# Decoder step with expert retrieval: two expert tables joined into one, gathered once a slot, and value rows weighted by diagonal matrices on TensorE

## The reference

```python
q = (xb @ w_q).reshape(PEER_BLOCK, PEER_HEADS, 2, PEER_DHALF).astype(F32)
s = jnp.einsum('nhpd,hpkd->nhpk', q, keys)
top_s, top_i = lax.top_k(s, PEER_TOPK)
...
idx = jnp.take_along_axis(cand_idx, best_j, axis=-1)
gsm = jax.nn.softmax(best_s, axis=-1)
act = jax.nn.gelu(jnp.einsum('nd,nhkd->nhk', xb, expert_u[idx]).astype(F32))
wts = (gsm * act).astype(xb.dtype)
return jnp.einsum('nhk,nhkd->nd', wts, expert_v[idx])
```

## Time and profile before

| | before |
|---|---|
| median of 3 runs | 2366.38 us (2363.53 to 2371.35) |
| span of the profiled execution | 2366.5 us |
| PE busy | 1659.4 us, 70% |
| DVE busy | 1552.5 us, 66% |
| ACT busy | 594.8 us, 25% |
| POOL busy | 1386.6 us, 59% |
| moved by DMA | 730.57 MB, of it 604.58 MB by the gathers |

### The profile page before, as it was taken

The page is one execution under the profiler, slowest core; times in us unless marked ns, Lnnn a source line. Parts: engine busy times, 40 slices in busy tenths (PEclk is TensorE's granted clock), DMA queues, the critical chain, the costliest instruction groups (busy, mean ns, idle before and its releaser), DMA issues. The chain is left out here.

```text
span 2366.5 us, 16881 instructions
## 1 busy us (share of the span) xinstructions
PE 1659.4 (70%) x4628; PEld 841.7 (36%) x4628; DVE 1552.5 (66%) x3174; ACT 594.8 (25%) x777; POOL 1386.6 (59%) x1231
## 2 busy tenths in 40 slices
PE   7999977888799999867754544555445556555545
PEld 3799863344345555523311111121111112111111
DVE  2450289989785666586777787587777556556554
ACT  1161222222642212322222222121222112221212
POOL 0000026565557776556666666766677886777784
PEclk9999998999799999887876666566666656765578
DMA  8766578999789999788988888988888988899996
GB/s 274 248 206 213 181 280 314 334 334 349 275 318 382 397 395 383 281 298 306 344 317 296 315 303 301 314 310 303 318 289 316 325 319 328 319 327 346 332 322 236
DMA packets 286556, 730.57 MB, mean 309 GB/s; under 512 B 22187, under 2 KB 135220, under 8 KB 286333
## 3 DMA queue, kind: packets, MB, share of 16 engines
q0 software_dynamic: 166032, 604.58, 70.5%
q1 hardware_dynamic: 119188, 123.91, 15.9%
q10 hardware_dynamic: 1250, 1.09, 0.2%
HBM read 726.43 MB, written 3.06 MB: 308 GB/s over the span
## 5 line engine op out<-in xcount | busy, mean ns | idle before, releaser
L689 PE MATMUL v_sum<-t_v_rows,t_ident 128*128 128x512 f32 (+1 forms) x1152 | 819.0, 853 | 649.2 <-DVE t_v_rows L1303 648.5
L479 POOL DMA_INDIRECT t_u_rows<-in_expert_u,t_step_idx x576 | 673.8, 1170 | 468.2 <-POOLq L478 336.5
L479 POOL DMA_INDIRECT t_v_rows<-in_expert_v,t_step_idx x576 | 681.7, 1184 | 178.3 <-issue 161.1
L1303 DVE SCALAR_TENSOR_TENSOR t_v_rows<-t_v_rows,t_wts 128x1024 f32<-128x1024 f32 x288 | 370.1, 1285 | 474.8 <-ACT t_v_rows L859 471.8
L689 PEld LDWEIGHTS v_sum<-t_v_rows,t_ident 128*128 128x128 f32 (+1 forms) x1152 | 266.0, 252 | 1156.5 <-DVE t_v_rows L1303 905.2
L859 ACT ACTIVATE t_v_rows<-t_v_rows,t_wts 128x1024 f32<-128x1024 f32 x288 | 330.5, 1147 | 1347.6 <-DMA t_v_rows<-in_expert_v,t_step_idx 1318.8
L601 PE MATMUL bank<-t_arena,t_weights 128*128 128x192 f32 (+1 forms) x2560 | 646.6, 411 | 8.2 <-issue 5.0
L601 PEld LDWEIGHTS bank<-t_arena,t_weights 128*128 128x128 f32 x2560 | 454.0, 192 | 205.3 <-issue 60.2
L1277 DVE CUSTOM_DVE_ANT_0 t_u_rows<-t_u_rows,t_arena 128x1024 f32<-128x1024 f32 x384 | 459.0, 1224 | 24.4 <-DMA t_u_rows<-in_expert_u,t_step_idx 20.5
L1277 DVE CUSTOM_DVE_ANT_0 t_u_rows<-t_u_rows,t_tok 128x1024 f32<-128x1024 f32 x192 | 227.9, 1222 | 10.2 <-DMA t_u_rows<-in_expert_u,t_step_idx 8.0
L470 POOL COPY t_step_idx<-t_idx 128x16 uint32<-128x16 uint32 x24 | 9.5, 421 | 308.9 <-DVEq L1263 308.8
(11 more groups left out here) (166 smaller groups left out, 910.8 us busy)
## 6 DMA issues: line engine op xcount, KB each, us to landing
t_weights<-in_w_in SPq DMA_DIRECT2D x40, 1024.0 KB, 6.0
t_weights<-in_w_ada SPq DMA_DIRECT2D x24, 1024.0 KB, 5.4
t_weights<-in_w_q SPq DMA_DIRECT2D x16, 1024.0 KB, 7.6
t_u_rows<-in_expert_u,t_step_idx POOLq DMA_INDIRECT x576, 6.2
t_v_rows<-in_expert_v,t_step_idx POOLq DMA_INDIRECT x576, 6.3
t_weights<-in_w_branch_a SPq DMA_DIRECT2D x8, 1024.0 KB, 10.5
t_weights<-in_w_branch_b SPq DMA_DIRECT2D x8, 1024.0 KB, 10.9
t_weights<-in_w_out SPq DMA_DIRECT2D x8, 1024.0 KB, 11.6
```

The lines of the kernel that those rows point to most:

```text
L479: pool.indirect_dma_start(out=rows[:, k % slots, :], out_offset=None, in_=source, in_offset=bass.IndirectOffsetOnAxis(ap=step_idx[:, table ...
L689: nc.tensor.matmul(v_sum[0:m, half], add, row[:, half], start=False, stop=False).then_inc(v_free, 1)
L1303: V.scalar_tensor_tensor(out=two, in0=one, scalar=wts[:, k:k + 1], in1=two, op0=ALU.mult, op1=ALU.add).then_inc(paired_done, 1)
```

## The change

`expert_u` and `expert_v` are joined on the host to one table of 16384 rows of 2048 floats (8 KB). One gather brings u and v of a slot into one of `NSLOT` = 8 buffers of 8 KB a partition, so 576 gathers take the place of 1152, and the 64 KB that the buffers take in a partition stand against 48 KB before (the scratch for DMA descriptors is set to 4096 B). There is no fetching of u a step ahead. For each pair DVE makes two dots and nothing else; ACT makes gelu of 2 numbers, two products with `gsm`, and two diagonal matrices (identity times weight) that are written over the used u rows; PE multiplies each v row by its diagonal matrix, so four matmuls of 128x512 a pair instead of two. The multiply-and-add on DVE (L1303), ACT's scaling of a row (L859) and DVE's `weigh` are gone. The stages of the dots ahead of stage A are gone as well; some units that stood ahead of the first pair (queries 12 to 15, the rows of tile 1, a norm, two choices) now stand in the first places of stage A, and the load of the second group's x is issued by ACT.

```diff
-NW, NU, NV, NBANK = 3, 4, 8, 6
+NW, NSLOT, NBANK = 3, 8, 6
...
-    start += [[u] for u in queries[:5] + [key, queries[5], pair] + queries[6:8] + [number] + queries[8:10]
-              + [key1, queries[10], dot[0], queries[11], pair1, queries[12], queries[13], queries[14], queries[15],
-                 ("tok", 1, 0), square, dot[1], number1, norm, ("ada", 0, 22), dot[2], key2, ("ada", 0, 23), dot[3], pair2]]
+    start += [[u] for u in queries[:5] + [key, queries[5], pair] + queries[6:8] + [number, queries[8], queries[9], key1, queries[10], queries[11], pair1]]
...
+    places[0] += [queries[12], number1]
+    places[1] += [queries[13], queries[14]]
+    places[2] += [queries[15], ("tok", 1, 0)]
+    places[3] += [square, key2]
+    places[4] += [norm]
...
+        uv_rows = sb("uv_rows", [P, NSLOT, 2 * D])
...
+        def diag_of(t, k):
+
+            return uv_rows[:, k % NSLOT, 0:NS if t == 0 else P]
...
+            def fetch_step(t, i, number, odd, first):
+
+                nc.gpsimd.tensor_copy(step_idx[:, odd, :], idx_of(t)[:, bass.ds(i * TOPK, TOPK)]).then_inc(idx_copied, 1)
+                pool.wait_ge(idx_copied, number + 1)
+                for k in range(TOPK):
+                    if k >= NSLOT or not first:
+
+                        pool.wait_ge(slot_free, 1)
+                        pool.sem_inc(slot_free, -1)
+                    pool.indirect_dma_start(
+                        out=uv_rows[:, k % NSLOT, :], out_offset=None, in_=A["expert_uv"],
+                        in_offset=bass.IndirectOffsetOnAxis(ap=step_idx[:, odd, k:k + 1], axis=0),
+                    ).then_inc(uv_in[k % NSLOT], 16)
...
+            def sum_pair(t, number, j):
                 m = rows_of(t)
-                add = ident2[:, :] if t == 0 else ident[:, :]
-                for j in pairs:
-                    pe.wait_ge(paired_done, number * PAIRS + (j + 1))
-                    row = v_rows[:, (2 * j + 1) % NV, :]
-
-                    for half in (slice(0, 512), slice(512, D)):
-                        nc.tensor.matmul(v_sum[0:m, half], add, row[:, half], start=False, stop=False).then_inc(v_free, 1)
+                pe.wait_ge(diag_done, number * PAIRS + (j + 1))
+                for k in (2 * j, 2 * j + 1):
+                    nc.tensor.matmul(v_sum[0:m, 0:512], diag_of(t, k), v_row(k)[:, 0:512], start=False, stop=False)
+                    nc.tensor.matmul(v_sum[0:m, 512:D], diag_of(t, k), v_row(k)[:, 512:D], start=False, stop=False).then_inc(slot_free, 1)
...
+            def weigh(t, number, j):
+
+                p = number * PAIRS + (j + 1)
+                two = slice(2 * j, 2 * j + 2)
+                act.wait_ge(dots_done, p)
+                nc.scalar.activation(gelus[:, two], dots[:, two], ACT.Gelu_apprx_tanh).then_inc(gelu_done, 1)
+                act.wait_ge(gelu_done, p)
+                nc.scalar.activation(wts[:, 2 * j:2 * j + 1], gelus[:, 2 * j:2 * j + 1], ACT.Copy, scale=step_gsm[:, 2 * j:2 * j + 1])
...
+                nc.scalar.activation(diag_of(t, 2 * j), one, ACT.Copy, scale=wts[:, 2 * j:2 * j + 1])
+                nc.scalar.activation(diag_of(t, 2 * j + 1), one, ACT.Copy, scale=wts[:, 2 * j + 1:2 * j + 2]).then_inc(diag_done, 1)
...
-                one, two = v_rows[:, k % NV, :], v_rows[:, (k + 1) % NV, :]
-                dve.wait_ge(v_in[k % NV], number * (16 * TOPK // NV) + 16 * (k // NV + 1))
-                dve.wait_ge(scaled_done, number * PAIRS + (j + 1))
-                V.scalar_tensor_tensor(out=two, in0=one, scalar=wts[:, k:k + 1], in1=two, op0=ALU.mult, op1=ALU.add).then_inc(paired_done, 1)
+                dve.sem_inc(gsm_done, 1)
+
+            def pair(t, number, j):
+
+                for k in (2 * j, 2 * j + 1):
+                    dve.wait_ge(uv_in[k % NSLOT], number * (16 * TOPK // NSLOT) + 16 * (k // NSLOT + 1))
+                    ins = V.tensor_tensor_reduce(out=u_row(k), in0=u_row(k), in1=h2_rows(t), scale=1.0, scalar=0.0, op0=ALU.mult, op1=ALU.add,
+                                                 accum_out=dots[:, k:k + 1])
+                ins.then_inc(dots_done, 1)
```

More of the change, by code:

```diff
@@ L176, in schedule @@
     places = [[] for _ in range(PAIRS * len(steps))]
-    later = [number2] + [u for t, y in ((0, 3), (1, 0), (1, 1), (1, 2), (1, 3)) for u in choice_units(t, y)]
-    deal(later, places, 0, CHOICE_PLACES)
-    spread(copied, places, 0, CHOICE_PLACES)
+    places[0] += [queries[12], number1]
[3 more added lines that the diff above has]
+    places[4] += [norm]
+    later = [("ada", 0, 22), pair2, ("ada", 0, 23), number2] + [u for t, y in ((0, 3), (1, 0), (1, 1), (1, 2), (1, 3)) for u in choice_units(t, y)]
+    deal(later, places, 5, CHOICE_PLACES)
+    spread(copied, places, 6, CHOICE_PLACES)
     queries, (key, pair, number) = query_units(1), choice_units(2, 0)
@@ L190, in between @@
             if after:
-                close = j == PAIRS - 1 and i == TILE_STEPS[t] - 1
-                return [("sum", "pair", t, (i, j))] + [("both", "final", t, 0)] * close
-            return [("pair", "pair", t, (i, j))] + [("both", "final", t - 1, j + 1)] * (t > 0 and i == 0 and j < 3)
+                return [("sum", "pair", t, (i, j))]
+            return [("pair", "pair", t, (i, j))] + [("both", "final", t - 1, j)] * (t > 0 and i == 0 and j < 4)
         return between
@@ L198, in schedule @@
     for t in group_tiles(1):
-        last = TILE_STEPS[t] - 1
+        last = TILE_STEPS[t]
         if PEELED[t]:
@@ L211, in schedule @@
             s += [("both", "loop", t, (PEELED[t], last))]
-        s += staggered([[] for _ in range(PAIRS)], pair_entries([(t, last)]))
-    s += [("both", "final", t, stage) for stage in (1, 2, 3)]
+    s += [("both", "final", t, stage) for stage in range(4)]
     return s
@@ L363, in trunk @@
         dve_step, coef_done, idx_done, rates_done = (sem(x) for x in ("dve_step", "coef_done", "idx_done", "rates_done"))
[L364 to L367 removed]
+        uv_in = [sem(f"uv_in{i}") for i in range(NSLOT)]
+        gsm_done, gsm_copied, idx_copied, dots_done, gelu_done, wts_done, diag_done, slot_free = (sem(x) for x in (
+            "gsm_done", "gsm_copied", "idx_copied", "dots_done", "gelu_done", "wts_done", "diag_done", "slot_free"))
         v_tile, v_read, yfin, ysq, ymean, ystd, yready, tails, out_done = (sem(x) for x in (
@@ L511, in _ @@
                     number = STEP0[t] + i
-                    after = following(t, i)
-                    if after and after[1] % (TILE_STEPS[after[0]] // 4) == 0:
-                        pool.wait_ge(idx_done, 4 * after[0] + 1 + 4 * after[1] // TILE_STEPS[after[0]])
-                    fetch_step(after, (t, i), number % 2, number)
+                    if i % (TILE_STEPS[t] // 4) == 0:
+                        pool.wait_ge(idx_done, 4 * t + 1 + 4 * i // TILE_STEPS[t])
+                    fetch_step(t, i, number, number % 2, number == 0)
                 if kind == "loop":
@@ L694, in _ @@
                     with pe.Fori(0, end - first) as i:
-                        sum_pairs(g, i + (STEP0[g] + first), range(PAIRS))
+                        for j in range(PAIRS):
+                            sum_pair(g, i + (STEP0[g] + first), j)
                 elif kind == "final":
@@ L1330, in _ @@
                         for j in range(PAIRS):
-                            pair(g, i + first, i + (STEP0[g] + first), j, g)
+                            pair(g, i + (STEP0[g] + first), j)
                 elif role == "pair":
-                    i, j = b
-                    next_tile = g if i + 1 < TILE_STEPS[g] else g + 1 if g + 1 < TILES else None
-                    pair(g, i, STEP0[g] + i, j, next_tile)
+                    pair(g, STEP0[g] + b[0], b[1])
                 elif role in ("make", "sum"):
                     continue
-                elif kind == "dots":
-                    for k in quarter(b):
-                        dot(0, 0, k)
                 elif kind == "ada":
```

121 lines of the change are left out of this document (31 added, 90 removed).

## The result

The changed kernel takes 2182.36 us (median of 4 runs, 2181.82 to 2185.64) against 2368.38 (4 runs) for the kernel before: a ratio of 0.9225, 95% interval 0.9203 to 0.9246, so 7.75% faster. The prediction said 2243, 5.2% faster. The profiled execution has a span of 2180.4 us.

The account below looks back on a forecast made before the run. POOL's gather issue was taken to bound stage B, PE and DVE stage A. After the change: 325 (start) + 861 (stage A) + 1036 (stage B) + 21 (end) = 2243 us, range 2120 to 2385 for 8 in 10.

Parts of the forecast that it names:

- What bounds stage B: In the last 192 pairs of the kernel before, POOL's gather issue was the bound: 199 of 205 us for 32 pairs.
- Stage B, 1036 us: The last 192 pairs: 991 us at the DMA engines' pace, plus 45 us for choices and queries.
- 5.16 us a pair: DMA pace for the last 192 pairs, the middle of 5.30 (396 GB/s) and 5.02 (418 GB/s).
- The choices: Choices and queries lengthen the last 192 pairs by 45 us, between 0 and 53, through DVE and the loading of weights.
- Stage A, 861 us: Pairs 0 to 95: PE's 827 us of work at a busy share of 0.96, between 827 and 950 us.
- Start and end: The first pair's sum stands at about 325 us; 21 us follow the last transfer's end.
- POOL's issue, 1.47 us: An 8 KB-row gather costs POOL 1.17 + 0.30 us as before, 2.9 us a pair; upper bound 2.64 us each.
- The ring: In the last 192 pairs each of eight buffers is held 15 to 17 us, where 20.6 are allowed.
- The rival of 23.6 us: Buffers held 23.6 us would set the pace of the last 192 pairs at 5.9 us each; total 2385 us; chance 0.13.
- The clock: In the last 192 pairs TensorE was counted on at 2.4 GHz; the sign was a PE clock above 0.85.
- The rival of 2659 us: TensorE stays at half clock: eight records take 7.56 us a pair in the last 192 pairs; chance 0.08.
- 358 GB/s: Rival: transfers in the last 192 pairs go no faster, 5.86 us a pair; total 2377 us, no gain; chance 0.05.

Follow-up runs that it names:

- light engines: The change with two 4 KB gathers a slot and each dot over half its row: 2296.75 us; with the value sum's right half also left out: 2191.49 us.
- the short gather at every second slot: The change, plus a second gather of 16 rows of 64 bytes, read by nothing, behind every second slot: 2197.05 us.

## Why the prediction was right, point by point

The direction, the places and the mechanism held; the sum was 61 us too high.

- **What bounds stage B.** Right, and shown by two steps that keep the 8 KB rows: POOL held by a filler takes back most of what one gather a slot gains (50 of 69 us in the last three parts), a second gather at every other slot, with POOL not full, next to none of it (4 us). One part of the argument was too simple: the prediction let the halved count do all of it, but 131 of the 250 us came with two gathers a slot still issued. In the one part with pairs alone that was compared, POOL's busy time fell by 20.8 us and the part by 18.6, so there it is POOL's time, by shorter issues (152.1 to 135.4 us) and fewer copies of indices (7.1 to 2.9); that the missing addition shortened the issues is likely, but no run took the addition alone away. The row that the prediction read on this was off by a little: that issue ended 0.82 us after the dot, not its full 0.94.
- **Stage B, 1036 us, measured 1014.** The mis-sized term is the pace, 5.16 us a pair: the parts of pairs alone, (156.7 + 164.4 + 156.6)/95.5, give 5.00, by the bound of 5.02 that the earlier trace rows gave for gathers alone. A short burst without other traffic was the better row, because that is what stage B then consists of. The choices cost 1014 - 191.5 x 5.00 = 56 us, 11 more than taken, and not only by DVE and the weights, as the prediction had it: with half of the sum left out they cost by the same count 984.6 - 191.5 x 4.965 = 34, so some 22 us of them are PE's.
- **Stage A, 861 us, measured 824.** The share of 0.96 was right (0.955); PE's work was 787 us and not 827. 36 of these 40 us lie in the sum: it kept PE busy 206.9 us in stage A before (388 records, 0.53 each) and 350.3 after (762, 0.46 each), 143 more where 179 were taken. The prediction priced the added records at 0.465 and left the old ones as they were, but the old ones were dearer and became cheaper too. Whether the clock did that, granted at 0.97 where those rows had 0.89 to 0.96, or the longer row of records, no run separates. The windows of `v_sum`, after and before (PE, PEld, ACT):

```profile
322.70:1146.90 824.20, 350.31 (x762) 129.65 (x763) 1.00 (x1) 0.97 0.84 302
376.60:1087.30 710.70, 206.88 (x388) 68.22 (x388) 1.02 (x1) 0.93 0.93 340
```

- **Start and end.** The first sum ran from 327.9 to 333.1 us (325 forecast), and 19.5 us follow the start of the last dot (21 forecast from the last transfer's end). Both fit.
- **POOL's issue, 1.47 us.** 1.175 + 0.30: the lower bound was right, twice the bytes cost POOL nothing.
- **The ring.** The hold of 15 to 17 us was measured as 16.1 to 17.2 with four slots. The rival of 23.6 us falls.
- **The clock.** 0.90 to 1.00 in stage B, above the 0.85 named. The rival of 2659 us needed half clock throughout and falls; PE was busy 117 to 128 of 157 to 164 us in the parts of pairs alone.
- **358 GB/s.** 417 were moved in the last part and 423 at the pace of its dots, so that rival falls. The Trainium skill, "HBM Reference", section "Specifications (TRN2)", has another figure: a core that streams alone measures well above that share, about 425 GB/s; the trace agrees.
- **ACT.** 1.45 us a pair in the timeline where 1.4 was taken; hidden, as forecast, beside the next rows' transfer.

What stays open: with two gathers of 4 KB rows and light engines POOL needs only 160 to 162 us of the last part and waits some 14 to 19 us for slots, and yet it takes 180 to 182. POOL is hardly fuller there than with the short gather at every second slot, which lost nothing, so POOL's time alone does not explain those two runs. Whether the shorter rows add something was not settled; with 8 KB rows no such remainder shows.

## What to carry to other kernels

POOL paid here for a gather by the issue, not by the byte: when its engine is full, join tables so that one issue brings all rows of an index, and count every issue stretched beside wide DVE operations as part of the same load. Once it has slack, the pace of the DMA engines may be next, and the best row for that pace was here a short window in which gathers ran alone at a full share. Where another engine bounds one stage and not the next, choose the form of the work stage by stage: PE's diagonal sum was hidden where the gathers bound (half of it left out gained 3.5 of 478 us in the three parts with pairs alone), and cost 55 us where PE did (stage A, 824 against 769). No run had the old sum in stage B.
